# A 16-expert layer on one core: the first ring slot refilled by units, the last expert interleaved with its combines, filler matmuls in TensorE's waits, the last quarter summed onto the residual in PSUM

## The reference, cut to what matters

```
def expert(args):
    xe, wgu, wd = args                                  # 32 x 1024, 1024 x 4096, 2048 x 1024
    gu = jnp.einsum('bcd,df->bcf', xe, wgu)
    ga, up = jnp.split(gu, 2, axis=-1)
    return jnp.einsum('bcf,fd->bcd', jax.nn.silu(ga) * up, wd)
...
x = x + ec_moe(rmsnorm_2(x, norm_ffn_g[layer]), router_w[layer], expert_w_gu[layer], expert_w_down[layer])
return rmsnorm_2(x, final_norm_g)
```

## Time and profile before

| what | value |
|---|---|
| time, three runs | 1514.47, 1514.93, 1515.52 us; median 1514.93 |
| profiled execution: its time | 1520.58 us |
| profiled execution: its span | 1518.8 us |
| TensorE busy | 1187.9 us (78%) |
| DVE, ACT, POOL busy | 444.8, 380.5, 88.2 us |
| DMA | 504.40 MB, mean 332 GB/s |
| mean granted TensorE clock | 0.872 of 2.4 GHz |

### The profile page before, as it was taken

One profiled execution on the slowest core, in us unless ns is written; L12 is line 12 of the kernel. 1 busy time (PEld: TensorE's weight loads), 2 busy tenths in 40 slices (PEclk: granted clock), 3 DMA queues, 4 the chain that ended last, 5 costly groups with the idle time before them and its releaser, 6 DMA issues.

```text
span 1518.8 us, 20004 instructions
## 1 busy us (share of the span) xinstructions
PE 1187.9 (78%) x8730; PEld 773.2 (51%) x8730; DVE 444.8 (29%) x872; ACT 380.5 (25%) x843; POOL 88.2 (6%) x97
## 2 busy tenths in 40 slices
PE   7999999999997997897757666666567667566665
PEld 6898989999976776443312322223223223123112
DVE  4565676554688855000000000000000000000002
ACT  4555566444555644100000000000000000000002
POOL 0000010000135412000000000000000000000001
PEclk9999999999998999887877877888887778788786
DMA  8345446464453259899999999999999999999995
GB/s 320 140 139 222 167 164 239 164 267 180 164 213 139 98 218 382 366 431 427 431 433 431 429 431 430 434 429 432 429 428 433 431 430 427 435 430 430 427 428 234
DMA packets 33767, 504.40 MB, mean 332 GB/s; under 512 B 4624, under 2 KB 5264, under 8 KB 8208
## 3 DMA queue, kind: packets, MB, share of 16 engines
q1 hardware_dynamic: 29808, 493.96, 78.1%
q10 hardware_dynamic: 3872, 9.16, 1.8%
HBM read 502.06 MB, written 1.05 MB: 331 GB/s over the span
## 4 chain that ended last, share of the span: by engine, by line
PE 65%; another core or an unknown queue 14%; DMA 8%; DVE 5%; issue 3%; ACT 3%; POOL 1%; ACTq 0%; POOLq 0%; DVEq 0%
PE PB L99 63%; DMA RING<-in_wgu_dram 3%; DMA RING<-in_wdn_dram 3%; PE PB L102 2%; DMA PIOTA<-in_piota_dram 1%; DVE SPL L108 1%; ACT SPH L105 1%; POOL SPL L108 1%; DVE SG L108 1%; ACT SG L105 1%; DVE CO L116 0%; POOL SM L136 0%; DVE AQK L108 0%; DMA X<-in_x_dram 0%
## 5 line engine op out<-in xcount | busy, mean ns | idle before, releaser
L99 PE MATMUL PB<-RING,XS 128*32 128x512 f32 x2048 | 333.6, 802 | 172.5 <-DMA RING<-in_wgu_dram 168.7
L99 PEld LDWEIGHTS PB<-RING,XS 128*32 128x32 f32 x2048 | 73.6, 139 | 386.5 <-DMA RING<-in_wgu_dram 205.3
L99 PE MATMUL PB<-RING,HHT 128*32 128x256 f32 x2048 | 162.6, 479 | 83.8 <-DMA RING<-in_wdn_dram 81.5
L108 DVE TENSOR_TENSOR SPL<-RAW,SPH 128x512 fp32r<-128x512 f32 x306 | 202.7, 721 | 39.2 <-ACT SPH L105 37.1
L99 PE MATMUL PB<-XTH,SPL 128*128 128x256 f32 x704 | 201.7, 287 | 0.0
L99 PE MATMUL PB<-XTH,SPH 128*128 128x256 f32 x704 | 199.2, 283 | 0.0
L99 PE MATMUL PB<-XTL,SPH 128*128 128x256 f32 x704 | 199.1, 283 | 0.0
L105 ACT ACTIVATE SPH<-RAW 128x512 fp32r<-128x512 f32 x340 | 186.4, 621 | 4.3 <-issue 1.8
L99 PEld LDWEIGHTS PB<-RING,HHT 128*32 128x32 f32 x2048 | 75.0, 135 | 153.2 <-DMA RING<-in_wdn_dram 87.2
L105 ACT ACTIVATE SG<-PB 128x512 f32<-128x512 f32 x16 | 9.6, 597 | 551.9 <-PE PB L99 551.9
L99 PEld LDWEIGHTS PB<-XTL,SPH 128*128 128x128 f32 x704 | 135.0, 192 | 0.5
(11 more groups left out here) (294 smaller groups left out, 1356.4 us busy)
## 6 DMA issues: line engine op xcount, KB each, us to landing
RING<-in_wgu_dram SPq DMA_DIRECT2D x56, 4096.0 KB, 52.9
RING<-in_wdn_dram SPq DMA_DIRECT2D x28, 4096.0 KB, 52.8
RAW<-in_wst_dram SPq DMA_DIRECT2D x85, 1024.0 KB, 4.9
RING<-in_wgu_dram SPq DMA_DIRECT2D x11, 2048.0 KB, 50.1
RING<-in_wdn_dram SPq DMA_DIRECT2D x7, 2048.0 KB, 19.8
RING<-in_wgu_dram SPq DMA_DIRECT2D x10, 1024.0 KB, 6.9
X<-in_x_dram SPq DMA_DIRECT2D x2, 512.0 KB, 6.7
MEM<-in_mem_dram ACTq DMA_DIRECT2D x1, 1024.0 KB, 7.3
```

The lines of the kernel that those rows point to most:

```text
L99: return pe.do(lambda e: e.matmul(out_, lhsT, rhs, start=start, stop=stop), after)
L108: return on.do(lambda e: e.tensor_tensor(out_, a, b, op), after)
```

## The change

Four things are edited.

1. The first slot's load for expert 1 is split into its four units: `ring_unit(q, w)` loads 1 MB as soon as unit `q` was read. For this `refill` in `expert_in` moves into the loop over the two banks.
2. In the last expert TensorE gets filler work: `keep_busy(b, n)` emits `n` float32 matmuls of the identity with itself, 128 x 128, into a bank that nobody reads. There are 16 of them behind each of k = 2 to 6, 10 behind k = 7, and 10 behind `expert_out` of m = 0 and of m = 1.
3. The last expert's `combine(m - 1)` and what follows it stand between the two halves (i = 0 and i = 1) of `expert_out(m)`.
4. The last quarter is not added by DVE: a float32 matmul of the identity with `X` starts the sum in PSUM, and the one-hot matmuls add to it. Tile 0 is squared by ACT from PSUM, tile 1 is copied and squared on DVE (`ttr`); the sums of both tiles go through one DVE add and one power on POOL. Of the four output DMAs, ACT issues two and SP two.

```
     def ring_load(e, g, after):
         slot = SLOT_OF[g]
-        note(e, g, 0, 4, [load(sp, RING[slot][:, :], weights_of(e, g), s_r[slot], 16 * e, after)])
+        note(e, g, 0, 4, [load(sp, RING[slot][:, :], weights_of(e, g), s_r[slot], 16 * (e - (g == 0)), after)])
+
+    def ring_unit(q, after):
+        slot = SLOT_OF[0]
+        c = slice(UNIT * q, UNIT * q + UNIT)
+        note(1, 0, q, 1, [load(sp, RING[slot][:, c], weights_of(1, 0)[:, c], s_second[q], 16, after)])
...
     def refill(n, w):
         e, i = divmod(n, 4 * NS)
         g, q = divmod(i, 4)
-        if e < 14:
+        if e == 0 and g == 0:
+            ring_unit(q, w)
+        elif e < 14:
             if q == 3:
                 ring_load(e + 1, g, w)
...
             for c in range(4):
                 w = mm(PB[b][32 * c:32 * c + 32, :], XS[e % 2][:, k, :], chunk_at[n][:, 512 * c:512 * c + 512],
                        k == 0, k == KD - 1, *chunk_in[n], xs_ok[e, k], *(held[b] if k == 0 else []))
-        refill(n, w)
+            refill(n, w)
...
     def expert_hidden(e, w):
+        if e == 15:
+            keep_busy(3, 10)
         a = act(SG[:, :], PB[0][:, :], ACT.Silu, w, st.get("sg"))
...
-    def expert_out(e, m, h):
+    def keep_busy(b, n):
+
+        for _ in range(n):
+            w = mm(PB[b][:, 0:P], ident, ident, True, True, *held[b])
+        return w
+
+    def expert_out(e, m, h, between=None):
...
+            if between and i == 0:
+                between()
         refill(n, w)
...
-            mm(PB[b][:, c], g[:, x], YL[m % 2][:, :], own or (e == 0 and m % 2 == 0), False, *y, st["g"], *held[b])
+            if own:
+                mm(PB[b][:, c], ident, X[:, t, T * m:T * m + T], True, False, x_last[t], *held[b])
+            mm(PB[b][:, c], g[:, x], YL[m % 2][:, :], e == 0 and m % 2 == 0, False, *y, st["g"], *held[b])
...
                 w = expert_in(e, k)
+                if e == 15 and 2 <= k < KD - 1:
+                    keep_busy(2, 16)
...
-    res = combine(15, 3, expert_out(15, 3, h))
-    a = [add_part(t, 3, t, res[t]) for t in range(2)]
-    q = [square(t, 3, a[t]) for t in range(2)]
+    ys = []
+    for m in range(4):
+        between = (lambda: finish_part(m - 1, ys[m - 1])) if m else None
+        ys.append(expert_out(15, m, h, between))
+        if m in (0, 1):
+            keep_busy(0, 10)
+    res = combine(15, 3, ys[3])
+    c = slice(3 * T, 4 * T)
+    last = [PB[t][:, T:2 * T] for t in range(2)]
+    q0 = act(SQ[0][:, :], last[0], ACT.Square, res[0], sq, scale=1.0 / 32, accum_out=ms_last[:, 0:1])
+    x1 = copy(X[:, 1, c], last[1], res[1])
+    q1 = ttr(SQ[1][:, :], X[:, 1, c], X[:, 1, c], 1.0 / D, 0.0, ALU.mult, ALU.add, ms_last[:, 1:2], x1, gu_done)
+    s2 = tt(total, total, ms_last, ALU.add, q0, q1, *summed)
     for t in range(2):
-        gained(t, 3, a[t], dve)
-        summed[t] = tt(total[t], total[t], ms[t][:, 3:4], ALU.add, q[t], summed[t])
-    r = [rsqrt(total[t], summed[t]) for t in range(2)]
+        yg[t].append(tt(YG[:, t, c], last[t], GF[:, c], ALU.mult, res[t], g_fin, gu_done))
+    r_ok = power(r_all, total, s2)
```

More of the change, by code:

```diff
@@ L279, in build @@
     IOTA = place("IOTA", [P, T], F32, at(29))
-    SQ = place("SQ", [P, T], F32, at(30))
+    SQ = [place(f"SQ{i}", [P, T], F32, at(30 - 15 * i)) for i in range(2)]
     GT = [place(f"GT{i}", [P, T], F32R, low(8.5 + i)) for i in range(2)]
@@ L818, in build @@
     s_fill = {}
+    s_second = [sem(f"s_second{i}") for i in range(4)]
     s_half = [sem(f"s_half{i}") for i in range(NS)]
@@ L845, in ring_half @@
         c = slice(2 * UNIT * h, 2 * UNIT * h + 2 * UNIT)
-        got = (s_half[slot], 16) if h else (s_r[slot], 16 * 15)
+        got = (s_half[slot], 16) if h else (s_r[slot], 16 * (15 - (g == 0)))
         note(15, g, 2 * h, 2, [load(sp, RING[slot][:, c], weights_of(15, g)[:, c], *got, after)])
@@ L1658, in build @@
     g_fin = load(act_l, GF[:, :], row("final_norm_g_2", D), sem("s_gf"), 16, gu_done)
-    ms = [small(4), small(4)]
-    total = [small(), small()]
+    ms = [small(3), small(3)]
+    ms_last, total, r_all = small(2), small(2), small(2)
     sq = None
-    yg, summed = [[], []], [None, None]
+    yg, summed, x_last = [[], []], [None, None], [None, None]
     def add_part(t, m, b, after):
@@ L1671, in square, with gained, finish_part @@
         nonlocal sq
-        sq = act(SQ[:, :], X[:, t, T * m:T * m + T], ACT.Square, a, sq, scale=1.0 / 32, accum_out=ms[t][:, m:m + 1])
+        sq = act(SQ[0][:, :], X[:, t, T * m:T * m + T], ACT.Square, a, sq, scale=1.0 / 32, accum_out=ms[t][:, m:m + 1])
         return sq
-    def gained(t, m, a, on):
+    def gained(t, m, a):
         c = slice(T * m, T * m + T)
-        yg[t].append(tt(YG[:, t, c], X[:, t, c], GF[:, c], ALU.mult, a, g_fin, gu_done, on=on))
-    for m in range(3):
-        res = combine(15, m, expert_out(15, m, h))
+        yg[t].append(tt(YG[:, t, c], X[:, t, c], GF[:, c], ALU.mult, a, g_fin, gu_done, on=pool))
+    def finish_part(m, y):
+        res = combine(15, m, y)
         for t in range(2):
@@ L1685, in build @@
                     q = square(t, i, a)
-                    gained(t, i, a, pool)
-                summed[t] = stt(total[t], ms[t][:, 0:1], EPS, ms[t][:, 1:2], ALU.add, ALU.add, q)
+                    gained(t, i, a)
+                summed[t] = stt(total[:, t:t + 1], ms[t][:, 0:1], EPS, ms[t][:, 1:2], ALU.add, ALU.add, q)
             elif m == 2:
                 a = add_part(t, 2, 5 + 2 * t, res[t])
-                add_part(t, 3, 5 + 2 * t, res[t])
-                gained(t, 2, a, pool)
-                summed[t] = tt(total[t], total[t], ms[t][:, 2:3], ALU.add, square(t, 2, a), summed[t])
-    res = combine(15, 3, expert_out(15, 3, h))
-    a = [add_part(t, 3, t, res[t]) for t in range(2)]
-    q = [square(t, 3, a[t]) for t in range(2)]
+                x_last[t] = add_part(t, 3, 5 + 2 * t, res[t])
+                gained(t, 2, a)
+                summed[t] = tt(total[:, t:t + 1], total[:, t:t + 1], ms[t][:, 2:3], ALU.add, square(t, 2, a), summed[t])
+    ys = []
[11 more added lines that the diff above has]
+    s2 = tt(total, total, ms_last, ALU.add, q0, q1, *summed)
     for t in range(2):
-        gained(t, 3, a[t], dve)
-        summed[t] = tt(total[t], total[t], ms[t][:, 3:4], ALU.add, q[t], summed[t])
-    r = [rsqrt(total[t], summed[t]) for t in range(2)]
+        yg[t].append(tt(YG[:, t, c], last[t], GF[:, c], ALU.mult, res[t], g_fin, gu_done))
+    r_ok = power(r_all, total, s2)
     n_out = 0
@@ L1703, in build @@
             c = slice(512 * i, 512 * i + 512)
+            line, y = (sp, YG[:, t, c]) if i else (act_l, YG[:, t, c])
             if i:
-                o = act(YG[:, t, c], YG[:, t, c], ACT.Copy, r[t][1], *yg[t], scale=r[t][0])
+                o = ts(y, y, r_all[:, t:t + 1], None, ALU.mult, None, r_ok, *yg[t])
             else:
-                o = ts(YG[:, t, c], YG[:, t, c], r[t][0], None, ALU.mult, None, r[t][1], *yg[t])
+                o = act(y, y, ACT.Copy, r_ok, *yg[t], scale=r_all[:, t:t + 1])
             n_out += 16
-            load(sp, out[t * P:(t + 1) * P, c], YG[:, t, c], s_out, n_out, o)
+            load(line, out[t * P:(t + 1) * P, c], y, s_out, n_out, o)
     sp.do(lambda e: e.nop(), [Load(s_out, n_out)])
```

## The result

The changed kernel takes 1519.67 us (median of 9 runs, 1518.16 to 1521.11) against 1515.35 us of the kernel before (9 runs beside them, 1514.47 to 1517.03). The ratio is 1.0024 with a 95% interval of 1.0015 to 1.0033: slower, by 4.3 us between the medians, 3.6 us by the ratio. The forecast was 1512.9 with a range up to 1516.7. One of those runs, 1543.32 us at a mean granted clock of 0.772, was in a slow state and is left out of the ratios.

A forecast was written before the change was run, and what follows sets the result against it. The prediction took the expert phase to be bound by its stream of weights. From the profiled 1520.58 us, -3.8 + 1.15 + 0.6 gave 1518.5, and 5.65 less for the median gave 1512.9, range 1509.0 to 1516.7.

The forecast's parts named there:

- term 3: Last expert's tail: interleaving alone gains 1.6 us, but with the fillers the last combine comes 1.15 us later.
- L: TensorE's lateness at k = 7 of the last expert, caused by fillers and clock: 4.65 us (3.75 to 6.9).
- term 1: Weight stream's gap at expert 0: loading by units brings all later loads 3.8 us earlier (2.5 to 5.1).
- Rival C: The stream's gain is lost to a new gap or to waits in experts 1 to 14: 1516.7 us, chance 0.15.
- Term 2: Fillers behind k = 2 to 6: 5.6 us per k against units every 4.89, 4.65 us late at k = 7.
- rival B: The last expert's fillers fit, at most 4.45 us per k, so TensorE is never late: 1509.2 us, chance 0.25.
- Rival D: Slower: the last expert's fillers run long at 1.2 GHz; 1520.5 us for three such blocks, chance 0.10.
- A: The main forecast, all four terms together: 1512.9 us, own range 1511.4 to 1515.5, chance 0.50.
- Term 4: The end behind the last combine: first output DMA 3.6 us behind it, a loss of 0.6 us (-0.3 to +0.9).

The follow-up runs named there:

- before_again: The kernel before, unchanged, run and profiled a second time: 1516.12 us against 1515.79 beside it, ratio 1.0000; its profiled execution took 1516.31 us.
- fitted: Kernel before with the first slot refilled by units and fewer fillers (8 behind k = 2 to 6, 4 at three later places): 1512.81 us, ratio 0.9973.
- refill_only: Kernel before with only the first slot's load for expert 1 split into units: 1514.98 us against 1515.79, ratio 0.9995.
- end_only: Kernel before with only the new handling of the last quarter, sums and output DMAs: 1516.83 us against 1516.12, ratio 1.0004.
- fillers_only: Kernel before with only the 110 fillers, the tens placed behind combine(0) and combine(1): 1521.71 us against 1515.79, ratio 1.0043.
- no_fillers: The changed kernel without any filler: 1517.04 us against 1516.12 of the kernel before, ratio 1.0004.
- no_blocks: The changed kernel without the five blocks of 16 fillers, the tens kept: 1516.92 us against 1516.12 of the kernel before, ratio 1.0005.
- fitted_two_slots: The fitted kernel with the second slot's load for expert 1 also by units: 1511.93 us against 1515.94 of the kernel before, ratio 0.9976.
- fitted_no_refill: The fitted kernel with the first slot loaded whole as before: 1514.62 us against 1515.94 of the kernel before, ratio 0.9985.

## Why the prediction was wrong

**The step that failed** is the baseline, in two places that belong together: "The median of the runs shown is 5.65 below the profiled time, so 1512.9", and term 3's "the gain against 1511.38 is 3.5 - L". I took the 5.65 us as something constant around the profile. Most of it was inside it: a tail of 28.1 us behind k = 7, with k = 7, m = 0 and m = 1 at 3.6 us each, where before_again shows 24.5. The profile of the changed kernel is only 1.44 above its median, so subtracting 5.65 took 4.2 us too much. The remaining 2.6 of the miss of 6.8 are the terms: the stream at k = 2 2.25 less early than the 3.8, L 0.65 larger, the end 0.5 longer, against an expert phase that happened to start 0.83 earlier (610.33, before 611.16).

The same sum on before_again's execution shows what it would have said: 1516.31 - 3.8 + 4.65 + (24.6 - 24.5) + 0.6 = 1517.9, less 0.5 (1516.31 against its median beside it, 1515.79) = 1517.4, slower by 1.6. With the sizes found below (term 1 2.3 instead of 3.8, L 5.3, end 1.1) it gives 1520.0, slower by 4.2; measured were 4.3. This sum was made after the result and takes its sizes from several profiles, so it shows that the account closes, no more.

**Term 1, the gap: right in kind, 3.8 predicted, about 2.3 found at k = 7.** The second load's landing came 3.2 earlier, not 3.8: issued at 622.9, it took 14.5 us to land, where 13.5 had been put. From the start of expert 0 to k = 7 are 868.8 to 870.4 us in the profiles of six kernels with the units and without blocks of 16 (mean 869.7), and 871.7 to 872.3 in five without either (mean 872.0). In fitted, 1.8 of this reached the last combine; the time of refill_only cannot tell. In the changed kernel's own execution it was less: k = 2 started 1456.48 - 610.33 = 846.15 behind expert 0, before 847.70, a gain of 1.55. Rival C (the gain lost) is thus true for two fifths of the 3.8 us in the means, for three fifths in the changed kernel's own execution.

**Term 2, the fillers: right.** 0.235 us for each filler, 5.62 a k as worked out, L = 5.3 against 4.65; the clock cost one slow k (3.22) and the start of the first block (4.18), and nothing more up to m = 2. The 32 passes of a block stand 0.118 us apart (3.76 / 32). The spacing of about 81 ns that the Trainium skill gives (TensorE: Matmul & The Clock Gate, "Back-to-back issue gap") is not what these float32 passes have, so rival B was out, and the reason to weigh the row above it held. Rival D fell too: from k = 3 to m = 2 the rows have the full clock's 1.92 us for 32 passes of 256 or 16 of 512 columns. Only m = 3 has slow rows again: 1.64 us for its first 16 passes, where m = 2's take 1.07. D's own price does not come out of its working: three blocks with their k at 11.3 us instead of 5.65 are 17 us more, not 8.5. Nor is A's own range that of its terms: 1514.93 less 3.0 and plus 0.2 is 1511.9 to 1515.1, not 1511.4 to 1515.5. Neither changes the forecast.

**Term 3, the tail: the chain right, what it was compared with wrong.** "The interleaving alone is worth the 1.6 us" is refuted twice: it costs 2.8 alone and 3.2 on top of fitted. The 1.6 is the distance from combine(2) to the last combine, 5.4 in the earlier trace rows less 3.8. In before_again, with the old order, that distance is 1507.12 - 1503.34 = 3.8 already, since m = 3 takes 1.93 us there and not 3.43: what I had put down to the interleaving was the clock of one execution. What the interleaving does is a price paid earlier, at combine(1), that now starts behind half of m = 2 and not in the wait ahead of it. In the earlier trace rows this wait did not exist, since the slow clock had filled it. The fillers' lateness then is not set off against a slow tail: 2.8 us in the changed kernel.

**Term 4, the end: 0.6 predicted (-0.3 to +0.9), 0.7 in end_only's profile (9.9 against 9.2), 1.1 in the changed kernel's** (1521.11 - 1510.83 = 10.3), where the last combine ran at 0.55 instead of 0.36 us. As a difference of times it stays within the interval of its ratio.

The medians of the single edits don't add up: refill -0.8, fillers +5.9, interleaving +2.8 and end +0.7 make 8.6, measured 4.3. Most of the difference is fillers_only, whose tens stand behind the combines: in the changed kernel they start while ACT and DVE still work on `YL`, m = 0, 1 and 2 start 4.3 and 5.1 us apart and not 6.0, and no_fillers against no_blocks, both without the blocks of 16, finds no cost of theirs. With the refill at the profiles' 2.3 and the blocks alone (2.6), the sum is -2.3 + 2.6 + 2.8 + 0.7 = 3.8 of 4.3. How much the blocks' lateness and the interleaving, which share one tail, take from each other was not tested.

## What to carry to other kernels

Before a sum is made on one profiled execution, hold its time against the median: a distance of some us can be one stretch of this execution, and the terms that touch that stretch need a second profile. Filler work keeps the clock for free only while it is shorter than the wait it stands in: 8 fillers (2.05 us) in a wait of 3 gained, 16 (3.84 us) lost; and the place counts: the tens cost nothing that could be told where they filled TensorE's wait for `YL`, and 3.2 us in all where they stood behind it. Work whose inputs are ready belongs ahead of an instruction that waits for a transfer, not behind it, even if the order behind looks smoother.

## What the runs showed of the hardware

**The stream ends at half rate.** In stretches of 2 us (columns as in the earlier trace rows) before_again and fitted_two_slots end their weights like this:

```profile
1494.00:1496.00 2.00, 1.88 (x24) 0.65 (x16) 0.00 (x0) 0.05 (x1) 0.00 (x0) 0.74 0.86 354
1496.00:1498.00 2.00, 0.71 (x4) 0.53 (x4) 0.88 (x3) 0.43 (x1) 0.00 (x0) 1.00 0.47 201
...
1500.00:1502.00 2.00, 2.00 (x24) 0.66 (x16) 0.54 (x2) 0.93 (x4) 1.37 (x2) 0.53 0.48 195
```

```profile
1490.00:1492.00 2.00, 1.75 (x32) 0.78 (x24) 0.00 (x0) 0.18 (x1) 0.00 (x0) 1.00 0.62 252
1492.00:1494.00 2.00, 1.04 (x9) 1.07 (x10) 1.01 (x3) 0.37 (x2) 0.00 (x0) 1.00 0.52 213
...
1496.00:1498.00 2.00, 1.41 (x28) 0.58 (x20) 0.67 (x3) 1.49 (x5) 1.42 (x2) 1.00 0.47 195
```

For 6 to 8 us before the last weights are in, the DMA share is about 0.5, at 200 instead of 431 GB/s. The trace has sixteen landings for each load, one for each DMA engine's part, and they show why: of the last load of before_again eight parts land from 1495.5 to 1496.7 and eight from 1501.9 to 1503.5. A load has landed when its last part has, and half of the engines are done 5 to 8 us before the others. This distance between a load's first and last part grows along the stream: in before_again 1.9 us at expert 1's second load, 8.0 at the end.

It also goes with what term 1 lost. Seen from the start of k = 0 the second load has landed after 27.3 us in the mean of six profiles whose first slot alone is loaded by units, and after 30.0 in seven without units, a gain of 2.7; the last weights have landed after 890.7 and 892.8 us, a gain of 2.2. In the changed kernel the distance is 3.1 us at the second load (1.9 in the kernel before) and 11.9 at the end (8.0). That an idle gap lets the engines that lag catch up is my reading and not shown: over the gap the distance goes from 2.2 to 0.7 us in before_again, but from 1.8 to 1.9 in the first profile of the same kernel. No experiment changed it.

**One kernel, 7 us of spread.** The 33 runs of the kernel before beside fitted_two_slots go from 1513.70 to 1520.65 us, the 9 of fitted_two_slots from 1511.00 to 1512.41. In the profiles of before the last expert has matmul groups of 1.92 and of 3.0 to 3.6 us in changing places; in those of fitted, fitted_no_refill and fitted_two_slots all from k = 3 on have 1.92 or 1.93. That the clock in the tail makes the runs above 1519 us fits this and their low mean clock. It does not explain the rare short runs: fitted_no_refill, whose tail is at the full clock in its profile, has one of 1509.38 us, 5.2 below its median, and the kernel before has three of 1510.5 to 1511.0. Their cause is open.
